# The denominator of the mLSTM cell: VectorE folds the normaliser's query product into the score weights, TensorE sums once

## What is computed

```
s   = einsum(qc, kc) * w_intra                      # scores of the chunk, weighted
num = einsum(s, vc) + w_inter * einsum(qc, C)       # C: the 512x512 state
den = sum(s, axis=2) + w_inter * einsum(qc, n)      # n: the normaliser state, 512 numbers
h   = num / max(abs(den), exp(-m_t))
C_new = decay * C + einsum(kc * wk, vc)
n_new = decay * n + einsum(wk, kc)
```

## Time and profile before

| | |
|---|---|
| Median of three runs | 2296.69 us |
| Time of the profiled execution | 2293.11 us |
| Its span, first to last instruction | 2291.3 us |
| Mean granted TensorE clock | 0.963 |
| TensorE busy (products) | 2155.5 us, 94% |
| VectorE busy | 1051.8 us, 46% |
| GpSimd busy | 485.9 us, 21% |
| Cell stage, all four heads | about 1560 to 2290 us of the span |

### The profile page before, as it was taken

How to read it: one execution, slowest core, us unless ns; L and a number is a source line. 1 busy time by engine, 2 the same in 40 slices (tenths; PEclk the granted TensorE clock), 3 DMA queues, 4 the chain that set the end, 5 groups by cost and what they waited for, 6 DMA issues and landing times. The chain is left out here.

```text
span 2291.3 us, 34691 instructions
## 1 busy us (share of the span) xinstructions
PE 2155.5 (94%) x12991; PEld 1879.6 (82%) x12991; DVE 1051.8 (46%) x1842; ACT 769.6 (34%) x1609; POOL 485.9 (21%) x479
## 2 busy tenths in 40 slices
PE   5999979989999999998999999976989989999998
PEld 4999967768999989997999899964668668658668
DVE  5222237846654305420543054215753753763762
ACT  3115648843332323322323233223422422431431
POOL 3000016622310001100100011012531531440540
PEclk8999979999999999999999999996998999999999
DMA  6631122014621332232213322227864664664672
GB/s 217 77 85 37 37 57 69 1 35 142 177 58 66 124 115 67 82 108 106 58 66 124 115 67 83 89 82 225 261 183 122 216 204 131 212 219 127 202 237 78
DMA packets 321878, 272.65 MB, mean 119 GB/s; under 512 B 57942, under 2 KB 268438, under 8 KB 321635
## 3 DMA queue, kind: packets, MB, share of 16 engines
q1 hardware_dynamic: 307838, 221.67, 32.3%
q10 hardware_dynamic: 13880, 48.77, 6.5%
HBM read 168.94 MB, written 102.40 MB: 118 GB/s over the span
## 5 line engine op out<-in xcount | busy, mean ns | idle before, releaser
L378 ACT ACTIVATE sb_whi<-sb_wraw 128x1024 fp32r<-128x1024 f32 x108 | 114.1, 1057 | 462.9 <-PE ps L399 382.9
L383 DVE TENSOR_TENSOR sb_wlo<-sb_wraw,sb_whi 128x1024 fp32r<-128x1024 f32 x108 | 138.1, 1279 | 281.0 <-ACT sb_whi L378 273.8
L399 PE MATMUL ps<-sb_h1h,sb_whi 128*128 128x360 f32 x1152 | 254.2, 329 | 6.6 <-issue 6.6
L399 PE MATMUL ps<-sb_h1l,sb_whi 128*128 128x360 f32 x1152 | 252.6, 327 | 0.0
L399 PE MATMUL ps<-sb_h1h,sb_wlo 128*128 128x360 f32 x1152 | 252.4, 327 | 0.0
L399 PEld LDWEIGHTS ps<-sb_h1h,sb_whi 128*128 128x128 f32 x1152 | 199.2, 189 | 9.3 <-issue 9.1
L399 PEld LDWEIGHTS ps<-sb_h1h,sb_wlo 128*128 128x128 f32 x1152 | 199.9, 188 | 0.0
L399 PEld LDWEIGHTS ps<-sb_h1l,sb_whi 128*128 128x128 f32 x1152 | 199.6, 189 | 0.0
L1060 POOL COPY sb_ctail<-sb_xr 128x3 f32<-128x3 f32 (+1 forms) x16 | 3.0, 188 | 711.8 <-DVE sb_xr L1193 711.8
L1781 PE MATMUL pm<-sb_cst,sb_qs 128*128 128x512 f32 x256 | 135.3, 611 | 0.9 <-DVE sb_swb L1972 0.5
L399 PE MATMUL ps<-sb_hh,sb_whi 128*128 128x360 f32 x480 | 115.6, 349 | 15.9 <-DVE sb_hl L421 12.7
(11 more groups left out here) (398 smaller groups left out, 4696.9 us busy)
## 6 DMA issues: line engine op xcount, KB each, us to landing
sb_scs<-state_mlstm_c SPq DMA_DIRECT2D x32, 1024.0 KB, 5.5
sample_mlstm_c<-sb_scs SPq DMA_DIRECT2D x32, 1024.0 KB, 5.2
sb_wraw<-mlstm_w_in SPq DMA_DIRECT2D x48, 512.0 KB, 3.8
sb_wraw<-swa_w_in SPq DMA_DIRECT2D x20, 512.0 KB, 3.9
scratch_ga<-sb_st ACTq DMA_DIRECT2D x16, 540.0 KB, 2.8
scratch_gb<-sb_st ACTq DMA_DIRECT2D x16, 540.0 KB, 3.7
scratch_v<-sb_st ACTq DMA_DIRECT2D x16, 540.0 KB, 2.7
scratch_q<-sb_st ACTq DMA_DIRECT2D x16, 540.0 KB, 2.7
```

Source lines behind the costliest of these rows:

```text
L378: act.activation(whi[q][:, :], wraw[q][:, :], ACT.Copy).then_inc(sem("w_hi"), 1)
L383: dve.tensor_tensor(wlo[q][:, :], wraw[q][:, :], whi[q][:, :].bitcast(F32), ALU.subtract)\
L399: last = pe.matmul(ps[s][:, g, 0:GRP], w[:, kk, c * P:(c + 1) * P], x[:, kk, g * GRP:(g + 1) * GRP], start=(kk == 0 and i == 0), stop=(kk ...
```

## The change

VectorE makes, for each chunk c > 0, a 128 x 128 tile `dsum` in four steps: the score weights plus, for k = 0 to 3, the weighted query piece k times column k of `nst` (a scalar for each partition). TensorE then makes one ones product of that tile instead of four one-column products and the ones product of the score weights. The four one-column products and their wait for `nst_done` go away; TensorE gets a wait for the fourth step. Two buffers of 128 x 128 are added.

```diff
@@ buffers
+    dsum = [rbuf(f"dsum{i}", [P, P]) for i in range(2)]
@@ cell_pe
                     pe.matmul(pm[0][0:n, :], qs[r][:, k, 0:n], cst[:, k, :], start=(k == 0), stop=False)
-                    if k == 0:
-                        pe.wait_ge(sem("nst_done"), due(NP * h + c))
-                    pe.matmul(SM[0:n, 0:1], qs[r][:, k, 0:n], nst[:, k:k + 1], start=(k == 0), stop=False)
                     if c > 1:
                         sample_update(c - 2, k)
-            pe.matmul(SM[0:n, 0:1], swb[r][0:n, 0:n], ones[0:n, 0:1], start=(c == 0), stop=True)
+            if c == 0:
+                pe.matmul(SM[0:n, 0:1], swb[r][0:n, 0:n], ones[0:n, 0:1], start=True, stop=True)
+            else:
+                wait_apart(pe, sem("dsum"), 4 * NBLK * h + 4 * c)
+                pe.matmul(SM[0:n, 0:1], dsum[r][:, 0:n], ones[:, 0:1], start=True, stop=True)
@@ cell_dve
+        def den_sum(c, k):
+
+            n, r = ROWN[c], c % 2
+            m = 4 * NBLK * h + 4 * (c - 1) + k
+            if k == 0:
+                wait_apart(dve, sem("qs_ready"), NCH * h + pre_no(c) + 1)
+                wait_apart(dve, sem("nst_done"), NP * h + c)
+                wait_apart(dve, sem("sw_done"), NCH * h + pre_no(c) + 1)
+            else:
+                wait_apart(dve, sem("dsum"), m)
+            more = swb[r] if k == 0 else dsum[r]
+            dve.scalar_tensor_tensor(dsum[r][:, 0:n], qs[r][:, k, 0:n], nst[:, k:k + 1], more[:, 0:n], ALU.mult, ALU.add)\
+                .then_inc(sem("dsum"), 1)
@@ cell_dve, the chunk loop
             if c > 0:
                 score_low(c)
+                den_sum(c, 0)
                 value_low(c)
+                den_sum(c, 1)
             if c > 1:
                 sample_state(c - 2, 0)
                 sample_state(c - 2, 1)
             if c > 0:
+                den_sum(c, 2)
                 key_low(c)
+                den_sum(c, 3)
             if c > 1:
                 sample_state(c - 2, 2)
                 sample_state(c - 2, 3)
```

## The result

The changed kernel takes 2402.88 us (median of 4 runs, 2394.09 to 2408.36), the kernel before 2295.28 beside it: a ratio of 1.0463, 95% interval 1.0438 to 1.0488, or +107 us. The prediction had the sign and the mechanism that starts the loss, but said 2329 with a top of 2347. Two thirds of the added time were not in its sum.

The account below looks back on a forecast made before the run. It took TensorE, then VectorE up to the row statistics, as each chunk's path, with the store loop nearly as long. Terms +13.0, +28.0, -3.5 and -4.5 gave +33, forecast 2329 us, range 2306 to 2347.

Parts of the forecast that it names:

- the new wait: TensorE's wait for VectorE's fourth step: about 1.2 us to the row statistics, plus 0.15 in heads 1 and 2.
- Case B: VectorE's first step takes the port before GpSimd's first operation; row statistics 0.93 us later per chunk, assumed for heads 0 and 3.
- the third rival: VectorE loses the port to GpSimd in all heads: +47, 2343 us; chance 0.22.
- the four operations in the way: GpSimd's TENSOR_TENSOR operations of the chunk, 1.27, 0.46, 1.28 and 1.28 us, covering the stretch of the new VectorE steps.
- The removed products: One-column products leaving TensorE: 0.22 us each, 0.88 a chunk, 28 us if TensorE stayed the path everywhere.
- The steps: Four new VectorE operations a chunk, each 0.35 us long and 0.27 from start to start, 1.08 us together.
- The port rule: VectorE operations with two SBUF tensors block behind GpSimd's TENSOR_TENSOR; a blocked new step ends 0.15 us after it.
- the rival's "about 2289": If the port does not bind, VectorE sets the row statistics at 5.83 us: sum -10.5, partly taken back; chance 0.12.
- The path of the stores: Sample-state store, load and chunk input loop, 12.9 us a chunk; its TensorE waits vanish in the longer chunks: -4.5 us.
- Chunk 1 was to gain 0.88: The chunk without sample pieces, where VectorE idles over four microseconds, gains in each of four heads: -3.5 us.
- the periods of 13.7 and 14.7: Spacing of row statistics after the change: 13.7 us in heads 0 and 3, 14.7 in heads 1 and 2, instead of 12.75.
- the signs named for being wrong: No long VectorE steps (up to 1.5 us) in the profile, or the sample pieces rather than the new steps carrying the delay.

Follow-up runs that it names:

- e5: Changed kernel with the four one-column products kept on TensorE, into a column nobody reads: 2367.74 us, ratio 1.0318.
- e9: Changed kernel with three unread TensorE products ahead of the third sample piece, none ahead of the wait for `dsum`: 2361.83 us, ratio 1.0297.
- e4: Changed kernel with unread TensorE products, seven ahead of the third sample piece and four ahead of the wait for `dsum`: 2356.9 us, ratio 1.0265.
- e3: Kernel before with only the four VectorE steps added, their tile never read, TensorE's program as before: 2345.91 us, ratio 1.0213.
- e2: Changed kernel without the VectorE steps, the one-column products gone too, normaliser's part left out: 2282.46 us, ratio 0.9933.
- e10: e2 with SyncE issuing the chunk-input load right behind the sample-state store, ahead of the wait for that store: 2263.93 us, ratio 0.9870.
- e11: Changed kernel, all steps moved ahead of `put`, weight split ahead of scores, chunk-input load issued ahead of the store's wait; complete: 2269.29 us, ratio 0.9894.
- e1: Changed kernel with the steps' second tensor read from the PSUM score bank, sum not accumulated: 2289.08 us, ratio 0.9961.
- e12: Kernel before with only SyncE's chunk-input load issued ahead of the wait for the sample-state store: 2291.19 us, ratio 0.9988.
- e7: Changed kernel with all four steps for the next chunk run behind `key_state`, before `put`; complete: 2287.39 us, ratio 0.9962.

## Why the prediction was wrong in size

**The step that failed** is in its part on the new wait: "From the end of step 3 to the row statistics TensorE needs about 1.2 us", priced from rows at full clock. It measured 2.16 (1630.19 to 1632.35), since TensorE ran at the lower level: L1789 took 0.45 instead of 0.22, L1794 1.63 instead of 0.82. More generally: of TensorE the prediction asked only when it would be late, never what standing still does to its clock. It had the stall in its own times (sample pieces at 4.05 behind steps 0 and 1) and gave no price to it. By e5, e9 and e4 that price is 33 to 45 us, the largest of the terms that the sum lacked.

**Who wins the port.** Case B was taken for heads 0 and 3, because VectorE could start step 0 0.03 us ahead. It does: in all 28 chunks with a full L1625 the record of step 0 starts 0.03 or 0.04 before GpSimd's, and in all 28 it loses and lasts 1.45 us. That is the third rival, "loses the port in all heads", +47; e3 measured +49. The prediction's reason for it, a wait of VectorE's own before step 0, did not come, not even in heads 1 and 2, where it had step 0 arrive late. What failed is its premise that the earlier start takes the port.

**The wait for step 3.** The sum had TensorE "level with VectorE" there. e5 over e3 gives about 24 us for that wait, and e4 over e3 12. Part of it is GpSimd's L1599, which the prediction did not count among the four operations in the way: in the chunk shown it adds 0.3 us to step 3, and over the launch it holds 14 of the 64 steps 2 and 3, some for 1.1 us. In the chunk of the earlier trace rows it started at 1633.27, behind the row statistics (1630.70); with these later it comes ahead of them.

**What held.** The removed products: 0.22 each, 0.88 a chunk, about 28 us (e2, e10). The steps: forecast 0.35, measured 0.34; 0.27 apart was too small only where each waits for the last (0.39 in e11). The port rule from the earlier trace rows carries over to 128 columns, and a blocked step ends 0.15 behind GpSimd, as worked out. The Trainium skill, page "SBUF — State Buffer", section "Who interferes with whom", states that rule; this trace agrees for GpSimd's TENSOR_TENSOR (1.46 and 1.32 us against 0.34 in e1), and e1 shows that one tensor in PSUM is enough to be free of it. That the holder keeps the port for its whole instruction does not hold for GpSimd's TENSOR_SCALAR: L1617, of 1.56 us, holds a step only until 0.83 us after its own start (the last section has the rows). The prediction had taken this operation to be harmless from the earlier trace rows, where the split starts 0.63 into it. Free of the port, the rival's "about 2289" was measured as 2289.08; that it fits so closely is luck, since what was added to its sum of 2286 was not priced. The path of the stores: its waits on TensorE vanished after the change, as forecast, and are worth about 4 us (e12).

**What else missed.** Chunk 1 was to gain 0.88. TensorE's first product to its ones product took 5.08 us before and 4.38 after, and it waited for step 3 there too, because step 1 met L1643 even in that chunk. "No idle of VectorE before L1987" was right, and the periods of 13.7 and 14.7 became 14.9 to 18.3. Of the signs named for being wrong, neither came; the forecast lacked one that would have said "TensorE slows down".

## What to carry to other kernels

Before work is moved to VectorE, look at what GpSimd runs in that stretch and from which memories each operand comes: a small operation with two SBUF tensors can take four times its length, while one operand in PSUM, or another place in the loop, costs nothing. When a change takes work from TensorE and makes it wait for the receiver, price the wait twice, once as time and once as the clock of what follows. The granted clock of the stretch is the sign; a longer mean of a matmul is one only where its neighbours are the same in both kernels. And when a saved microsecond does not show, look at the queue that feeds the loop: here half of the gain lay behind one load that stood behind the wait for a store.

## What the runs showed of the hardware that was not expected

- **Less work, lower clock, more time.** With stalls of 1.90 us in six of seven chunks the granted clock was 0.84; with 1.35 (e3) and 1.21 (e9) it was 1.00, and with 1.35 and the new wait behind it (e5) 0.95. No idle time of TensorE in those seven chunks of the kernel after was longer than 1.91 us. Three unread products, which fill 0.7 us of the stall, are worth 38 us in 28 chunks.
- **The first record does not own the port.** Step 0 starts 0.03 to 0.04 us ahead of L1625 and loses it in 28 of 28. Of nine steps that start 0.02 to 0.19 ahead of L1599, seven kept their 0.34, and L1599 grew from 1.27 to as much as 1.46 instead; two, both 0.04 ahead, were held for 1.45. Behind it by 0.05 to 0.15, the step was held in eight of eight. Step 0 starts 0.09 before the operation ahead of it has ended, but so does step 2, so that does not tell them apart. What does is open.
- **GpSimd's TENSOR_SCALAR holds the port for its first part alone.** In the kernel after, six steps start 0.12 to 0.42 us into L1617, and all end 0.83 us after its start, though it lasts 1.56. Steps that start 0.57 us or more into it take 0.33 to 0.35, here and in all 24 cases of e7. One of the six:

```profile
1713.39 1.56 POOL L1617 TENSOR_SCALAR sb_kwz<-sb_k,sb_blkm 96x512 fp32r<-96x512 f32 x1
1713.52 0.70 DVE L2032 SCALAR_TENSOR_TENSOR sb_dsum<-sb_qs,sb_nst,sb_dsum 128x128 f32<-128x128 f32 x1
```

- **A held operation is cheaper than its length.** It ends 0.14 to 0.16 us behind GpSimd's whether it was held for 0.1 or for 1.1 us.
